# Modulation and other 1024-wide vectors: loaded once as sixteen rows and spread by TensorE, instead of sixteen broadcast loads

## The chip, the cores and the metric

The kernel runs on one core of a Trainium2 chip. The time is the device time of one launch in microseconds (us); the kernel before has a median of 4399.28 us over three runs (4392.77 to 4406.4). The profiled execution took 4396.59 us, of which the profile's span covers 4394.8 us.

## The reference

Two layers of a diffusion backbone run over 128 context tokens and 512 latent tokens (640 rows of width 1024, float32; five tiles of 128 tokens, tile 0 context, tiles 1 to 4 latents). Layer 0 is a mixer (attention and RWKV), layer 1 a Conformer convolution module. Each layer ends with PEER, an expert retrieval: eight heads pick sixteen experts each for every token, so 128 experts of 16384, and each expert has a row `u` and a row `v` of 1024 floats. What this change touches are the vectors of 1024 that are the same for every token:

```python
sp1, cp1, gp1, sp2, cp2, gp2 = modulation(c_ctx[None, :], mod_w[layer], mod_b[layer])   # context
ss1, cs1, gs1, ss2, cs2, gs2 = modulation(c, mod_w[layer], mod_b[layer])                # latents
...
yp = mixer_odd(hp, *prm)                      # ends with "@ w_pw2 + b_pw2"
xp = xp + gp1 * yp
hp = modulate(rmsnorm(xp, norm_g[layer, 1]), sp2, cp2)     # h * (1 + scale) + shift
xp = xp + gp2 * peer(hp, *pprm)
y_prompt = rmsnorm(xp, final_g)
```

and the same for the latents. `peer` gathers `u_tab[eidx]` and `v_tab[eidx]`: sum over the 128 picks of gate * gelu(u . x) * v.

## The kernel before

`phase_mixer_even` (the first 885 us) computes layer 0's mixer and stores all modulation vectors in a DRAM tensor, `K.modrows` (two streams by twelve vectors of 1024). `phase_trunk` does the rest. Its backbone is ten jobs: PEER of layer 0 for tiles 0 to 4 (jobs 0 to 4) and of layer 1 for the same tiles (jobs 5 to 9). A job is 128 picks. For each pick GpSimd issues an indirect DMA that gathers one 8 KB row (u and v) for each of 128 tokens, 1 MB in all, into one of the eight slots of `ring` (L1602). VectorE takes the dot product with h (L1733), ScalarE makes gelu, weight and a diagonal matrix (L1893, L1898, L1904), TensorE multiplies the diagonal with the v half and accumulates over the job in PSUM (L2300 to L2303), and that frees the slot: GpSimd waits for it (`used`) before it issues the next gather.

Everything else of the trunk runs beside the picks, in order written out by hand: a `Side` is a generator that yields ticks, and each engine runs its sides up to tick r before its own work of pick r. VectorE does so at every pick, ScalarE and TensorE at every second. So a step at tick 40 on TensorE stands behind TensorE's pick 39, and a step at tick 42 on VectorE behind its dot product of pick 41. SyncE, which issues the ordinary loads, has no picks: it runs through its sides as far as its semaphore waits let it, and whatever it waits for holds every later load of its list.

The vectors of 1024 are used by VectorE with tokens on partitions, so each must be present on all 128 partitions. Before, each is a DMA with `partition_broadcast(P)`, a read of 128 times 4 KB from DRAM. There are sixteen:

- four into `nrows`, a part of the ring, at the trunk's start (`load_row`, L152): scale and shift of layer 0's PEER for both streams. `modulate_all` on VectorE (L1636, L1638) waits for them, tile 0 for two and tile 1 for two, and makes h of the five tiles.
- four into `grow` (L1554): the gate of PEER, for jobs 0, 1, 5 and 6, used in `add_up` (L1744, L1746) at tick 2 of the next job. For jobs 1, 5 and 6 SyncE waits for `summed` before it.
- one of `cv_b_pw2` and three of gate, scale and shift for tile 0 into `lrow` (L1537, L1539), in job 4, among the loads of `w_pw2`; and three of the latents into the same places (L1544), behind a wait for tile 0's h.
- `final_g` into `lrow` at the end of job 8 (L1584), used in `finish` (L1846).

The step of layer 1 between convolution and PEER is `post(p)`, in jobs 4 (tiles 0 and 1), 6 (tiles 2 and 3) and 8 (tile 4). TensorE multiplies by `w_pw2` in eight blocks at ticks 24 to 38 (L2235); each block's weights are one load of 512 KB into one of two buffers `wq`. Then VectorE adds the bias (`mix`, tick 41, L1818), multiplies by the gate (L1821), adds to x (L1824), after the norm applies scale (L1834) and shift (L1837), and TensorE transposes (tick 52, L2244). The second tile of a pair follows `later` ticks behind: 12 in job 4, 4 in job 6. Then come sixteen query blocks with a load of 512 KB each (L1511).

At the trunk's start ScalarE squares all five tiles and takes five roots (L1882, L1886), the last root waiting for VectorE's work on tile 2; only then does it copy the transposed h out of PSUM (`turned`, L2031), TensorE makes the context tile's queries (L2109) and scores (L2122), VectorE picks the first head's experts (`select`), and GpSimd starts its first gather.

## Time and profile before

| | |
|---|---|
| median of three runs | 4399.28 us |
| profiled execution | 4396.59 us |
| its span | 4394.8 us |
| mixer phase | 0 to 885 us |
| trunk up to the first gather | 887 to 919 us |
| ten jobs | 936 to 4388 us |
| TensorE busy, VectorE busy | 72%, 62% of the span |
| mean DMA rate over the span | 342 GB/s |

How to read the rows further down. PE is TensorE's matmuls, PEld its weight loads, DVE VectorE, ACT ScalarE, POOL GpSimd, SP SyncE; SPq is SyncE issuing a DMA. A line of the page cuts the span into 40 slices, with the busy share in tenths. A line of the table of stages holds: stretch and its length; busy time and instructions of PE, PEld, DVE, ACT, POOL; the granted TensorE clock (1.00 is 2.4 GHz, 0.50 is 1.2 GHz); the DMA engines' mean busy share; and GB/s moved. The stretches for jobs begin with the first dot product of each job. A line of the timeline holds start, length, engine, line, operation, output<-inputs, shape, count, and in brackets how long the engine had been idle and what released it. The profile records a float32 matmul as two instructions, a transpose as one; a count of matmuls in a row is of such records. A line of DMA issues holds destination<-source, the issuing queue, count, size of each and the median time from issue to landing.

### The profile page before, as it was taken

Reading aid. Unit: us, or ns where it says so; the run is one execution under the profiler, and the core shown is the slowest. Engines: PE = TensorE matmul, PEld = TensorE weight load, DVE = VectorE, ACT = ScalarE, POOL = GpSimd, SP = SyncE. Lnnn points to the kernel's source line nnn. Section 1 sums busy time; section 2 is a strip of 40 time slices with the busy share of each in tenths; the row PEclk is TensorE's granted clock in tenths of the full one; section 3 lists DMA queues with packets and bytes.
Section 4 is the critical chain, followed back from the end, with each engine's and each line's share of the span. In section 5 each row is a group of like instructions: output and inputs, shape, how many; then the busy total and the mean of one; then the engine's idle time right before and its main releaser. Section 6 shows DMA issues by size and latency. Waiting matters only on the chain.

```text
span 4394.8 us, 68645 instructions
## 1 busy us (share of the span) xinstructions
PE 3150.5 (72%) x25323; PEld 1501.5 (34%) x25323; DVE 2743.9 (62%) x6925; ACT 1604.0 (36%) x4949; POOL 1471.2 (33%) x1298
## 2 busy tenths in 40 slices
...
DMA  5153000179999999999999999999999999999998
GB/s 227 53 209 123 15 7 4 49 287 367 406 401 421 421 421 414 420 419 418 406 417 390 398 419 420 419 418 418 394 418 420 421 420 414 419 419 419 412 421 336
DMA packets 228988, 1505.07 MB, mean 342 GB/s; under 512 B 32198, under 2 KB 33313, under 8 KB 58289
## 3 DMA queue, kind: packets, MB, share of 16 engines
...
q10 hardware_dynamic: 442, 0.12, 0.0%
...
## 4 chain that ended last, share of the span: by engine, by line
DMA 46%; PE 16%; DVE 8%; ACT 5%; issue 3%; POOL 2%; SPq 0%; ACTq 0%; POOLq 0%; PEldq 0%; DVEq 0%
DMA t_ring<-in_peer_uv,t_eidx 44%; PE t_ps L2300 9%; DVE t_ring L1733 6%; POOL t_ring L1602 2%; PE t_ps L2206 2%; ACT t_dg L1904 1%; DMA t_wq<-in_cv_w_pw 1%; ACT t_wgt L1898 1%; PE t_ps L2109 1%; PE t_ps L2188 1%; PE t_ps L2235 1%; PE t_ps L2265 1%; ACT t_wgt L1893 1%; PE t_ps L2301 0%; DVE t_early L1796 0%
## 5 line engine op out<-in xcount | busy, mean ns | idle before, releaser
L1602 POOL DMA_INDIRECT t_ring<-in_peer_uv,t_eidx x1280 | 1463.7, 1143 | 2890.7 <-PE t_ps L2303 1828.7
L2300 PE MATMUL t_ps<-t_ring,t_dg 64*64 64x512 f32 x2560 | 1573.6, 746 | 1037.6 <-ACT t_dg L1904 1006.5
L1733 DVE SCALAR_TENSOR_TENSOR t_ring<-t_ring,t_hring 128x1024 f32<-128x1024 f32 x1024 | 1255.1, 1226 | 792.2 <-DMA t_ring<-in_peer_uv,t_eidx 789.8
L2303 PE MATMUL t_ps<-t_ring,t_dg 64*64 64x512 f32 x2560 | 1591.3, 754 | 0.0
L2302 PE MATMUL t_ps<-t_ring,t_dg 64*64 64x512 f32 x2560 | 1591.0, 753 | 0.0
L2301 PE MATMUL t_ps<-t_ring,t_dg 64*64 64x512 f32 x2560 | 1590.7, 753 | 0.0
L2300 PEld LDWEIGHTS t_ps<-t_ring,t_dg 64*64 64x64 f32 x2560 | 345.7, 156 | 2036.8 <-issue 2005.0
L1893 ACT ACTIVATE t_wgt<-t_dots 128x2 f32<-128x2 f32 x640 | 130.2, 204 | 1954.8 <-DVE t_ring L1733 1954.1
L1733 DVE SCALAR_TENSOR_TENSOR t_ring<-t_ring,t_early 128x1024 f32<-128x1024 f32 x256 | 314.8, 1230 | 248.3 <-DMA t_ring<-in_peer_uv,t_eidx 248.2
L1904 ACT ACTIVATE t_dg<-t_eye,t_wgt 128x64 f32<-128x64 f32 x1280 | 376.1, 340 | 1.4 <-ACT t_wgt L1898 0.9
L2303 PEld LDWEIGHTS t_ps<-t_ring,t_dg 64*64 64x64 f32 x2560 | 346.8, 156 | 0.0
L2301 PEld LDWEIGHTS t_ps<-t_ring,t_dg 64*64 64x64 f32 x2560 | 346.6, 156 | 0.1
L2302 PEld LDWEIGHTS t_ps<-t_ring,t_dg 64*64 64x64 f32 x2560 | 346.4, 156 | 0.0
L1898 ACT ACTIVATE t_wgt<-t_wgt,t_gate 128x1 f32<-128x1 f32 x1280 | 307.3, 286 | 40.0 <-DVE t_gate L1708 14.5
L2206 PE MATMUL t_ps<-t_early 128*128 128x256 f32 (+1 forms) x930 | 188.3, 355 | 0.0
L2206 PEld LDWEIGHTS t_ps<-t_early 128*128 128x128 f32 x930 | 153.2, 193 | 68.3 <-ACT t_early L1960 38.5
L318 PE MATMUL fr_ps<-ev_hT,ev_wring 128*128 128x512 f32 x336 | 174.3, 601 | 0.0
L2188 PE MATMUL t_ps<-t_early,t_wg 128*128 128x256 f32 (+1 forms) x768 | 154.9, 355 | 5.5 <-DMA t_wg<-in_cv_w_pw 3.2
L1893 ACT ACT_TABLE_LOAD x116 | 148.8, 1283 | 12.6 <-DVE t_ring L1733 10.6
L2265 PE MATMUL t_ps<-t_early,t_wq 128*128 128x256 f32 (+1 forms) x768 | 152.7, 354 | 0.0
L2188 PEld LDWEIGHTS t_ps<-t_early,t_wg 128*128 128x128 f32 x768 | 127.0, 194 | 64.7 <-issue 44.2
L1960 ACT ACTIVATE t_early<-ident,vec 128x128 f32<-128x128 f32 x465 | 145.1, 387 | 1.5 <-PE t_ps L2206 0.6
...
## 6 DMA issues: line engine op xcount, KB each, us to landing
...
t_ring<-in_peer_uv,t_eidx POOLq DMA_INDIRECT x1280, 13.7
...
ev_qk<-in_ab_w_out SPq DMA_DIRECT2D x1, 4096.0 KB, 12.1
...
```

The costliest lines, as they stand in the source:

```text
L1602: pool.indirect_dma_start(ring[:, place[n], :], None, table, bass.IndirectOffsetOnAxis(ap=eidx[:, s % 2, r:r + 1], axis=0)).then_inc(row_i ...
L1733: V.scalar_tensor_tensor(ring[:, place[n], 0:D], ring[:, place[n], 0:D], 1.0, h_of(j), ALU.mult, ALU.mult, accum_out=dots[:, j % 2, r:r + ...
L1893: nc.scalar.activation(wgt[:, r:r + 2], dots[:, j % 2, r:r + 2], ACT.Gelu).then_inc(S["gelu_done"], 1)
L1898: nc.scalar.activation(wgt[:, r + b:r + b + 1], wgt[:, r + b:r + b + 1], ACT.Copy, scale=gate[:, j % 2, r + b:r + b + 1]).then_inc(S["wgt_ ...
L1904: nc.scalar.activation(dg[:, n % DIAGS, :], eye[:], ACT.Copy, scale=wgt[:, r + b:r + b + 1]).then_inc(S["diag_set"], 1)
L2188: last = nc.tensor.matmul(banks[:, 4 + b % 2, 2 * a * P:2 * a * P + N], wg[:, a, k, :], rhs, start=(k == 0), stop=(k == KD - 1))
L2206: nc.tensor.matmul(tiles_of(banks[:, 4 + b % 2, :], p), diag[:, n % BATCH, :], windows(p, b, w), start=(w == 0), stop=(w == CONVW - 1)).th ...
L2265: last = nc.tensor.matmul(tiles_of(banks[:, 6 + b % 2, :], p), wq[:, n % 2, k, :], both[:, k, 0:E, :], start=(k == 0), stop=(k == KD - 1))
L2300: nc.tensor.matmul(straight[low], diagonal[low], row[low, 0:512], **ends)
L2301: nc.tensor.matmul(straight[high], diagonal[high], row[high, 0:512], **ends)
L2302: nc.tensor.matmul(crossed[high], diagonal[low], row[low, 512:D], **ends)
L2303: nc.tensor.matmul(crossed[low], diagonal[high], row[high, 512:D], **ends).then_inc(S["used"], 1)
```

## The change

`load_rows` reads the sixteen vectors once, one per partition, into a tile `rows` of 16 partitions, in six small DMAs at the trunk's start. Where a vector is needed on 128 partitions, TensorE multiplies a column of the identity, repeated 128 times as the stationary operand (16 x 128), with `rows` (16 x 512, twice), which leaves the vector on all partitions in PSUM. VectorE reads it there; only the gate of PEER is copied by ScalarE into `grow`. The bias of `w_pw2` is added by two more matmuls per tile into the same accumulation. As VectorE can read one operand from PSUM, ScalarE copies the product of `w_pw2` to SBUF (`product`) first. Ticks and semaphores are laid out anew, the query blocks of job 4 start at tick 66 instead of 72 and those of job 8 have a step of 3 from tick 66. At the start the transposes use two banks in turn instead of four, since the spread rows hold the others, and the latents' rows are spread after the transposes of tile 0.

```diff
+ROWS = 16
+def row_at(stream, layer, kind):
+    return 7 * stream + (kind + 1 if layer else kind - 3)
+def load_rows(eng, K, rows, sem):
+    for s in range(2):
+        for layer, first, at in ((0, 3, 0), (1, 2, 3)):
+            src = K.modrows[s, (layer * 6 + first) * D:(layer * 6 + 6) * D].rearrange("(r d) -> r d", d=D)
+            eng.dma_start(rows[7 * s + at:7 * s + at + 6 - first], src).then_inc(sem, 16)
+    eng.dma_start(rows[14:15], K.io["cv_b_pw2"]).then_inc(sem, 16)
+    eng.dma_start(rows[15:16], K.io["final_g"].rearrange("(a d) -> a d", a=1)).then_inc(sem, 16)
...
-    later = lambda p, e: (12, 4, 0)[p] * e
-    query_tick = lambda p, b: (72 + 3 * b, 66 + 3 * b, 60 + 7 * b // 2)[p]
-    ahead = lambda p: (12, 14, 14)[p]
+    later = lambda e: 4 * e
+    query_tick = lambda p, b: 66 + 3 * b
+    gate_tick = lambda j: 14 if j else 96
...
-        turned_bank = lambda n: (0, 1, 4, 5)[n % 4]
+        turned_bank = lambda n: n % 2
...
+        def after_product(p):
+            return sorted((at + later(e), n, kind, e) for n, (kind, at) in enumerate((("scale", 44), ("gate", 40), ("shift", 50), ("turn", 54)))
+                          for e in range(len(PAIRS[p])))
...
# SyncE
-                        if k == 2 and p == 0:
-                            sp.dma_start(lrow[:, 3, :], io["cv_b_pw2"][0].partition_broadcast(P)).then_inc(S["lrow_in"], 16)
-                            for a, kind in enumerate((2, 4, 3)):
-                                sp.dma_start(lrow[:, a, :], mod_row(0, kind).partition_broadcast(P)).then_inc(S["lrow_in"], 16)
-                    if p == 0:
-                        yield 51
-                        sp.wait_ge(S["h2_done"], 1)
-                        for a, kind in enumerate((2, 4, 3)):
-                            sp.dma_start(lrow[:, a, :], mod_row(1, kind).partition_broadcast(P)).then_inc(S["lrow_in"], 16)
-                def gate_row(j, tick):
-                    yield tick
-                    if j:
-                        sp.wait_ge(S["summed"], j)
-                    sp.dma_start(grow[:], mod_row(tile(j), 5, j // NT).partition_broadcast(P)).then_inc(S["grow_in"], 16)
-                for s in range(2):
-                    for j, kind in enumerate((4, 3)):
-                        load_row(sp, K, nrows[:, s, j, :], s, 0, kind, rows_in[s])
+                load_rows(sp, K, rows, S["rows_in"])
-                    if s == JOBS - 2:
-                        sp.wait_ge(S["h2_done"], NT)
-                        sp.dma_start(lrow[:, 0, :], io["final_g"].partition_broadcast(P)).then_inc(S["g_in"], 16)
...
# VectorE
                         if t < 2:
-                            dve.wait_ge(rows_in[t], 32)
-                        V.scalar_tensor_tensor(h_of(t), x[:, t, :], rstd[:, t:t + 1], nrows[:, stream(t), 0, :], ALU.mult, ALU.mult).then_inc(S["scaled"], 1)
+                            dve.wait_ge(S["nrows_spread"], 2 * (t + 1))
+                        V.scalar_tensor_tensor(h_of(t), x[:, t, :], rstd[:, t:t + 1], ps[:, 2, :], ALU.mult, ALU.mult).then_inc(S["scaled"], 1)
...
-                    yield 41 + later(p, e)
-                    dve.wait_ge(S["w_done"], p + 1)
-                    dve.wait_ge(S["lrow_in"], 16 * (7 if i else 4))
-                    m = own(V.tensor_tensor(y, ps[:, 2 + e, :], lrow[:, 3, :], ALU.add))
-                    yield 42 + later(p, e)
-                    after_own(m)
-                    m = own(V.tensor_tensor(y, y, lrow[:, 0, :], ALU.mult))
-                    yield 43 + later(p, e)
-                    after_own(m)
+                    yield 42 + later(e)
+                    dve.wait_ge(S["product_out"], i + 1)
+                    dve.wait_ge(S["post_spread"], 3 * PAIRS[p][0] + spread_at(p, "gate", e))
+                    V.tensor_tensor(y, product, ps[:, 1, :], ALU.mult).then_inc(S["gate_read"], 1)
+                    yield 43 + later(e)
+                    dve.wait_ge(S["gate_read"], i + 1)
                     V.tensor_tensor(x[:, i, :], x[:, i, :], y, ALU.add).then_inc(S["mixed"], 1)
...
+                    dve.wait_ge(S["post_spread"], 3 * PAIRS[p][0] + spread_at(p, "scale", e))
+                    V.scalar_tensor_tensor(h_of(j), x[:, i, :], rstd[:, n:n + 1], ps[:, 2 + e, :], ALU.mult, ALU.mult).then_inc(S["scale_read"], 1)
+                    yield 52 + later(e)
+                    dve.wait_ge(S["scale_read"], i + 1)
+                    dve.wait_ge(S["post_spread"], 3 * PAIRS[p][0] + spread_at(p, "shift", e))
+                    V.tensor_tensor(h_of(j), h_of(j), ps[:, 1, :], ALU.add).then_inc(S["h2_done"], 1)
...
# ScalarE
+                def gate_row(j, n):
+                    for a in range(2):
+                        yield gate_tick(j) + 4 * a + 2
+                        act.wait_ge(S["gate_spread"], 2 * n + a + 1)
+                        if j:
+                            act.wait_ge(S["summed"], j)
+                        nc.scalar.copy(grow[:, a * 512:(a + 1) * 512], banks[:, 3, :]).then_inc(S["gate_set"], 1)
...
+                        yield 40 + later(e)
+                        if e:
+                            act.wait_ge(S["gate_read"], i)
+                        else:
+                            act.wait_ge(S["w_done"], p + 1)
+                        nc.scalar.copy(product, ps[:, 2 + e, :]).then_inc(S["product_out"], 1)
...
# TensorE
-                        if n >= 4:
-                            pe.wait_ge(S["hT_done"], n - 3)
+                        if n >= 2:
+                            pe.wait_ge(S["hT_done"], n - 1)
...
+                def spread(row, outs):
+                    for a, out in enumerate(outs):
+                        last = nc.tensor.matmul(out, ident[0:ROWS, row:row + 1].to_broadcast([ROWS, P]), rows[:, a * 512:(a + 1) * 512], start=True, stop=True)
+                    return last
+                def norm_rows(s):
+                    for a, kind in enumerate((4, 3)):
+                        spread(row_at(s, 0, kind), (banks[:, 4 + 2 * a, :], banks[:, 5 + 2 * a, :])).then_inc(S["nrows_spread"], 1)
+                def gate_row(j, n):
+                    row = row_at(stream(tile(j)), j // NT, 5)
+                    for a in range(2):
+                        yield gate_tick(j) + 4 * a
...
+                        nc.tensor.matmul(banks[:, 3, :], ident[0:ROWS, row:row + 1].to_broadcast([ROWS, P]), rows[:, a * 512:(a + 1) * 512],
+                                         start=True, stop=True).then_inc(S["gate_spread"], 1)
+                def final_row():
+                    yield 4
+                    pe.wait_ge(S["hTb_done"], NT)
+                    spread(15, (banks[:, 4, :], banks[:, 5, :])).then_inc(S["g_spread"], 1)
...
+                    for e in range(E):
+                        for a in range(2):
+                            last = nc.tensor.matmul(ps[:, 2 + e, a * 512:(a + 1) * 512], ident[0:ROWS, 14:15].to_broadcast([ROWS, P]),
+                                                    rows[:, a * 512:(a + 1) * 512], start=False, stop=True)
+                    last.then_inc(S["w_done"], 1)
+                    for tick, _, kind, e in after_product(p):
+                        yield tick
+                        i = members[e]
+                        if kind == "gate":
...
+                            spread(row_at(stream(i), 1, 2), (banks[:, 2, :], banks[:, 3, :])).then_inc(S["post_spread"], 1)
+                        elif kind == "scale":
+                            pe.wait_ge(S["gate_read"], i + 1)
+                            spread(row_at(stream(i), 1, 4), (banks[:, 4 + 2 * e, :], banks[:, 5 + 2 * e, :])).then_inc(S["post_spread"], 1)
+                        elif kind == "shift":
+                            pe.wait_ge(S["gate_read"], members[-1] + 1)
+                            if e:
+                                pe.wait_ge(S["h2_done"], i)
+                            spread(row_at(stream(i), 1, 3), (banks[:, 2, :], banks[:, 3, :])).then_inc(S["post_spread"], 1)
...
+                pe.wait_ge(S["rows_in"], 16 * 6)
+                norm_rows(0)
                 turn(0, 2)
+                norm_rows(1)
```

## Rows read from the trace of the kernel before

**Rows 1.** The page: span, DMA busy tenths in 40 slices, the chain by engine.

```profile
span 4394.8 us, 68645 instructions
DMA  5153000179999999999999999999999999999998
...
DMA 46%; PE 16%; DVE 8%; ACT 5%; issue 3%; POOL 2%; SPq 0%; ACTq 0%; POOLq 0%; PEldq 0%; DVEq 0%
```

**Rows 2.** Busy time by stage, for jobs 3, 4, 6 and 7.

```profile
1972.90:2316.70 343.80, 256.37 (x1609) 130.57 (x1604) 256.64 (x676) 177.46 (x541) 146.89 (x128) 0.90 1.01 414
2316.70:2685.60 368.90, 257.06 (x1465) 118.50 (x1461) 235.44 (x589) 128.86 (x419) 150.01 (x129) 0.88 0.99 404
...
3029.40:3389.60 360.20, 259.94 (x1464) 118.36 (x1468) 236.62 (x589) 127.49 (x419) 147.49 (x128) 0.88 1.00 411
3389.60:3712.60 323.00, 209.03 (x1338) 83.03 (x1330) 242.27 (x658) 143.52 (x500) 145.91 (x127) 0.81 1.01 420
```

**Rows 3.** DMA issues of the whole span, with time to landing.

```profile
t_ring<-in_peer_uv,t_eidx POOLq DMA_INDIRECT x1280, 13.7
...
out<-at_kvtok SPq DMA_DIRECT2D x2, 64.0 KB, 1.7
```

**Rows 4.** SyncE's timeline in job 4, the loads around `w_pw2`.

```profile
2372.77 0.43 SPq L1537 DMA_DIRECT2D t_lrow<-in_cv_b_pw  x1
2373.24 1.43 SPq L1539 DMA_DIRECT2D t_lrow<-modrows  x3
2377.90 41.01 SPq L1535 DMA_DIRECT2D t_wq<-in_cv_w_pw  x5
```

**Rows 5.** Tile wq, 2300 to 2440 us: its matmuls, idle time until loads.

```profile
L2235 PE MATMUL t_ps<-t_wq,t_early x64: 592/592/1222, 2368.7 to 2429.7; 128*128 128x512 f32 x64
...
  DMA t_wq<-in_cv_w_pw: 36.2, 7
```

**Rows 6.** The same, 3020 to 3150 us (job 6).

```profile
  DMA t_wq<-in_cv_w_pw: 12.1, 9
```

**Rows 7.** VectorE's timeline in job 4, the first step of `mix`, both tiles.

```profile
2430.38 1.23 DVE L1818 TENSOR_TENSOR t_early<-t_ps,t_lrow 128x1024 f32<-128x1024 f32 x1 [6.19 <-PEq L2239]
...
2470.69 1.23 DVE L1818 TENSOR_TENSOR t_early<-t_ps,t_lrow 128x1024 f32<-128x1024 f32 x1 [9.22 <-DMA t_lrow<-modrows]
```

**Rows 8.** Busy time in stretches of 10 us of job 4.

```profile
2400.00:2410.00 10.00, 8.95 (x26) 3.46 (x27) 5.57 (x12) 1.63 (x8) 1.15 (x1) 0.67 0.76 301
...
2470.00:2480.00 10.00, 3.69 (x16) 0.89 (x16) 9.31 (x26) 2.07 (x10) 2.60 (x2) 0.58 0.89 340
```

**Rows 9.** Tensor work of 512 columns: timeline around 918 us, clock 1.00.

```profile
917.70 10.57 PE L2109 MATMUL t_ps<-t_ring,t_wq 128*128 128x512 f32 x24 [1.04 <-ACT t_ring L2031]
```

**Rows 10.** Timeline of the trunk's start, all engines.

```profile
886.96 1.75 SPq L152 DMA_DIRECT2D t_ring<-modrows  x4
...
892.48 1.28 DVE L1636 SCALAR_TENSOR_TENSOR t_early<-x,t_rstd,t_ring 128x1024 f32<-128x1024 f32 x1 [2.13 <-DMA t_ring<-modrows]
...
895.08 1.97 PE L2103 MATMUL t_ps<-ident,t_early 128*128 128x128 f32 x8 [12.61 <-DVE t_early L1638]
...
895.22 1.28 DVE L1636 SCALAR_TENSOR_TENSOR t_early<-x,t_rstd,t_ring 128x1024 f32<-128x1024 f32 x1
...
900.69 1.05 ACT L2031 COPY t_early<-t_ps 128x512 f32<-128x512 f32 x2
...
910.31 0.49 DVE L1650 MAX8 t_top<-t_early 128x8 f32<-128x128 f32 x2 [4.47 <-ACT t_early L2053]
...
919.20 1.02 POOL L1602 DMA_INDIRECT t_ring<-in_peer_uv,t_eidx  x1 [909.68 <-DVE t_eidx L1693]
```

**Rows 11.** The chain in order of time, job 9: dot products, next gather.

```profile
4152.23 1.25 DVE t_ring L1733 x2
...
4158.37 14.91 DMA t_ring<-in_peer_uv,t_eidx
```

**Rows 12.** Busy time 902 to 904 us, with the granted clock.

```profile
902.00:904.00 2.00, 2.00 (x10) 2.00 (x11) 1.96 (x3) 0.00 (x0) 0.00 (x0) 0.50 0.02 6
```

76 lines of the change are left out of this document (44 added, 32 removed).

## Prediction

> **What bounds the kernel now.** I read the page first. In the 40 slices the DMA digits are 7 or less up to slice 9 and 9 in slices 10 to 39, and DMA is the largest part of the chain, 46% [rows 1]. So there are two parts: a mixer phase that the change leaves alone, and the trunk from 887 us on. Next, the table by job. Job 7 has no ordinary loads: 128 picks in 323.0 us, DMA share 1.01 at 420 GB/s. Job 3 has sixteen loads of 512 KB beside the same picks and takes 343.8 us, also at full share. The difference, 20.8 us, is 1.30 us for a load; 524,288 bytes at 420 GB/s are 1.25 us. Against 323.0 us TensorE has 209 us and VectorE 242 us of work in job 7 [rows 2]. The trunk is bound by bytes: a load that is taken out of a job gives its 1.25 us back, and an operation added on TensorE or ScalarE costs nothing as long as ring slots come free in time. How much time there is for that: a gather lands 13.7 us after its issue [rows 3], while at 420 GB/s its 1 MB takes 2.5 us, so some five gathers are queued. The engines could be late by several microseconds before DMA runs dry.
>
> Job 4 breaks the rule. It has 29 ordinary loads (6 of `w_pw2`, 16 for the queries, 7 into `lrow`), so 323.0 + 29 * 1.25 = 359.3 us were due, and it took 368.9, at a share of 0.99. Job 6, with 25 loads and due at 354.3, took 360.2 [rows 2]. Job 4 loses 9.6 us, job 6 5.9.
>
> **The loads that go.** Four of the sixteen stand at the trunk's start, before the gathers; they are not byte savings. Twelve stand in jobs: seven in job 4, one each for the gates of jobs 0, 1, 5 and 6, and `final_g` in job 8. 12 * 1.25 = 15.0 us; at 1.30 it would be 15.6. A lower bound leaves out the load of job 0, the one job I don't take as byte-bound throughout: 13.8. I take 15.0.
> The Trainium skill (DMA: Bandwidth & Descriptors, Anatomy of one DMA) gives a DMA about 2.0 us plus bytes / 436e3. By that fixed part each load would be worth 3.2 us, 38 us in all. The trace doesn't agree: sixteen loads cost 20.8 us, not 51 [rows 2]; the fixed part is hidden while other transfers are queued.
>
> **Job 4's stalls.** The four loads of 512 KB into `lrow` are issued together, at 2372.8 to 2374.7 us, right ahead of the remaining blocks of `w_pw2`, which take until 2418.9 [rows 4]. TensorE then sits 36.2 us for `wq` in this stretch [rows 5], against 12.1 us for the same work of job 6 [rows 6]. VectorE waits 6.2 us behind it at the first step of `mix`, and for the second tile 9.2 us for the latents' rows [rows 7]. DMA runs partly empty at both places: shares of 0.76 and 0.89 in stretches of 10 us [rows 8], 2.4 + 1.1 = 3.5 us. That is about what job 4 loses more than job 6 (9.6 - 5.9 = 3.7). With the `lrow` loads gone I take -4 us. Ends: 0, if what is late next (the blocks of `w_pw2`, as in job 6) stalls as long; -9.6, if job 4 comes to what is due. SyncE also stops waiting for `summed` and for tile 0's h; the loads behind those waits go out earlier, with the same bytes, and job 6's blocks of `w_pw2` can be there before their tick. I give that nothing.
>
> **The new work beside the picks.** A float32 matmul is two records: 64 records for the 32 matmuls of job 4's `w_pw2` [rows 5]. 24 records of 512 columns take 10.57 us at a clock of 1.00 [rows 9], so a matmul takes 0.88 us there and 1.76 at 0.50. Per tile of `post` there are 2 for the bias and 6 for gate, scale and shift, 40 in five tiles; with 8 for PEER's gates and 2 for `final_g` 50 in all, 44 to 88 us of TensorE over jobs in which it has over 70 us free each [rows 2]. ScalarE gets five copies of 1024 columns and eight of 512, by 1.05 us for two of 512 [rows 10] 9.5 us. VectorE loses five additions of 1.23 us [rows 7], 6.2 us. As busy time all this lies under the DMA: zero.
>
> The waits are another matter. VectorE now waits at tick 42 (gate, spread by TensorE at tick 40, two picks or 5 us before), at 48 (scale, tick 44) and at 52 (shift, tick 50). From the end of a dot product to the next gather lie 4.9 us with two picks' matmuls between (4158.37 - 4153.48) [rows 11]; the two matmuls of a spread add 1.8 to 3.5. So the shift is there 6.7 to 8.4 us after dot 49, while VectorE comes 5.0 after it: a wait of 1.7 to 3.4 us. For the first gate, tick 38 also holds the last block of `w_pw2` and the bias, 7 us for a pair, and ScalarE waits for `w_done` before its copy, with its weights and diagonals behind it; for the second gate TensorE has scale and gate in a row. I put these two waits at 5 us each and the two shifts at 2.5: 15 us for a pair, about half for tile 4, 37 in all, less 6.2 us of additions. Behind VectorE's wait stand its dot products, and with them every slot. Of a pair's 15 us most is hidden: the 6.2 and 9.2 us waits of job 4 cost 3.5 us of DMA together [rows 7, 8]. At that ratio, 3.5 / 15.4, 37 us would cost 8.4; less the relief, I take +6. Ends: 0 (TensorE comes in time) and +25 (30.8 us, most of it felt, because the waits stand within sixteen picks).
>
> **The start.** Here nothing covers. Before, VectorE begins tile 0 at 892.48 us, 5.5 us after the first issue, and tile 1 at 895.22 [rows 10]. Now six issues of 0.44 us (four took 1.75 [rows 10]) end at 889.6, and a small load lands after 1.7 us [rows 3]: the rows are there at 891.3. TensorE makes four matmuls, 3.5 us at a clock of 1.00, 7.0 at 0.50. VectorE's tile 0 takes 2.6 us, TensorE transposes (1.97 us for eight [rows 10], or half), then spreads the latents' rows (3.5 or 7.0). Fast: 891.3 + 3.5 + 2.6 + 1.0 + 3.5 = 901.9, 6.7 us later than 895.2. Slow: 891.3 + 7.0 + 2.6 + 2.0 + 7.0 = 909.9, 14.7 later. The delay arrives at the first gather: ScalarE copies the transposes, at 900.69, only after its last root, which waits for VectorE's tile 2; then come queries, scores, the selection from 910.31 and the gather at 919.20, each waiting for the one ahead [rows 10]. VectorE's own end of the five tiles (about 906 us) has 4.5 us of slack before 910.31 and moves with the rest. The granted clock was 0.50 at 902 to 904 us, when the queries began [rows 12]. I take 0.50 for the first four matmuls in part, 5.5 us, and 1.00 from then on: 891.3 + 5.5 + 2.6 + 1.0 + 3.5 = 903.9, +8.7. The queries then run at 1.00 too, and the first of them, sixteen records, takes 1.8 instead of 3.5 us: -1.5. So +7; ends 5 and 15. Two banks instead of four for the latents' transposes lie behind the chain to the first gather: zero, or 1 us.
> The Trainium skill (TensorE: Matmul & The Clock Gate, Part 1: The HAM clock gate) says that the array runs at 1.2 GHz after idling until it has been kept busy. By that alone the first spread would be the slow one, 7.0 us, and the start +8.5.
>
> **The sum.** -15.0 - 4 + 6 + 7 = -6 us on the profiled execution's 4396.59, so 4390.6. This execution lies 2.7 us under the median of the runs; for the median, 4399.3 - 6 = 4393.3, given as 4393.
>
> **Rivals.** (1) More comes back: job 4 loses nothing any more (-9.6 instead of -4), job 6 gains 3 us from earlier loads, no new wait is felt (0) and the start costs 5: -15.0 - 9.6 - 3 + 5 = -22.6, 4377. For it: SyncE is released from four waits. Against it: job 6 loses 5.9 us without any `lrow` load.
> (2) Slower than before: the handoffs at ticks 38 to 58 of jobs 4, 6 and 8. If the waits of a pair add up to more than the queued gathers hold (five, of 2.5 us), DMA runs dry at each of the five tiles by 7 us: 35 in place of the 6, so +23, 4422. It makes the kernel slower from (6 + 6) / 5 = 2.4 us of lost DMA time a tile on. For it: such waits emptied the DMA before [rows 7, 8], and now four stand close together. Against it: the longest of them, 9.2 us, lost 1.1.
> (3) The loads weren't what the jobs paid for; they filled gaps that gathers can't use. Then the twelve give 0: -4 + 6 + 7 = +9, 4408. Against it: job 3 against job 7 [rows 2].
> (4) A load holds the DMA engines for a fixed time besides its bytes: 1.7 us, what a small load takes [rows 3]. Then each of the twelve gives 1.7 us more, 20.4 in all: -26.4, 4373. Against it: job 3 against job 7, 1.30 us for a load with everything in it [rows 2]. This is the rule of the Trainium skill's DMA page named above.
>
> **How the numbers follow.** Forecast 0.65, rival 1 0.12, rival 2 0.13, rival 3 0.07, rival 4 0.03. About 0.3% of the time, 13.2 us, is what a measurement of this kernel can tell from no change. The forecast's bounds, -15.6 - 9.6 + 0 + 5 = -20 and -13.8 + 0 + 25 + 15 = +26 at the outside, put 0.09 of its 0.65 past -13.2 and 0.05 past +13.2. So faster 0.12 + 0.03 + 0.09 = 0.24, slower 0.13 + 0.05 = 0.18, same 0.58. The range that leaves out 2 in 10 reaches at the low end almost to rival 1, 4378, at the high end past rival 3, 4412.
>
> **What would show it.** The table by job: job 4 at 350 to 358 us, jobs 0, 1 and 5 about 1.2 us shorter, job 7 at 323. The first gather at 924 to 929 us. TensorE's wait for `wq` in job 4 near 12 us. VectorE idle until TensorE or ScalarE at the gate's product, some 5 us each. I would be wrong if jobs with one load less stayed as long as before, if DMA shares fell under 0.9 at ticks 38 to 58 of jobs 4, 6 and 8, or if the first gather came before 922 or after 935 us.

## The result, and the profile after

The changed kernel has a median of 4406.39 us, the kernel before, in runs beside it, 4398.19. The ratio is 1.0021, 95% interval 1.0014 to 1.0028: slower by 9.2 us (8.2 by the medians), where 6 us faster was forecast. The time lies in the stated range, and the difference within the 0.3% (13.2 us) that the prediction took for the least that can be told from no change. With 22 runs of each kernel the interval is 0.07% to either side, so the difference is clear of zero; in the experiments, with 4 to 12 runs, it is 0.08 to 0.15%. The sign was wrong, and the two terms that make it so can be named. The profiled execution took 4404.7 us, 8.1 more than that of before.

The page (span, DMA busy tenths in 40 slices, the chain by engine):

```profile
span 4402.9 us, 68889 instructions
DMA  5152000159999999999999999999999999999998
...
DMA 41%; PE 21%; DVE 8%; ACT 4%; issue 4%; POOL 2%; SPq 0%; ACTq 0%; POOLq 0%; PEldq 0%; DVEq 0%
```

Against [rows 1] the chain has five hundredths less of DMA and five more of TensorE. Slice 9 is emptier: the gathers begin later. All slices after it are as full as before, which says that the page is too coarse for what follows.

A correction first, which holds for [rows 2] as well: the stretches there start 11.7 us after each job's first dot product, not with it, and so does the "936" of the table of times (the first dot product is at 924.7 us). Both ends of a stretch are off by the same amount, so the lengths, on which everything rests, are those from first dot product to first dot product. The table of after is cut in the same way, 11.9 us behind. Also, the DMA issues of job 6's stretch are 27 ordinary loads, not 25 (16 for the queries, 10 of `w_pw2`, one for the gate); at 1.25 us each 356.8 us were due there and 3.4 were lost, not 5.9.

Busy time by stage after (columns as in [rows 2]), jobs 3, 4, 6 and 7:

```profile
1986.10:2330.00 343.90, 258.37 (x1606) 131.88 (x1602) 256.92 (x676) 175.45 (x541) 152.82 (x128) 0.89 1.01 414
2330.00:2694.20 364.20, 283.04 (x1496) 125.71 (x1492) 233.17 (x587) 129.25 (x420) 150.50 (x128) 0.85 0.99 402
...
3037.00:3400.10 363.10, 283.27 (x1500) 126.65 (x1493) 233.02 (x587) 130.18 (x421) 143.85 (x128) 0.87 0.99 404
3400.10:3723.10 323.00, 214.95 (x1342) 84.64 (x1346) 244.78 (x665) 145.24 (x506) 144.55 (x128) 0.79 1.01 420
```

Jobs 3 and 7, which the change hardly touches, are as long as before within 0.2 us. Job 4 has 24 loads for 29 and is 4.7 us shorter; 6.25 were due for the bytes alone. Job 6 has 24 for 27 and is 2.9 us longer. The rest, from first dot product to first dot product: job 0 +4.6 us (its gate load is gone, but it has three loads more, 1 MB of keys and two of weights that waited for `summed` in job 1 before), job 1 -6.1, job 5 -1.0, job 8 -1.3, jobs 2 and 9 unchanged. In sum the ten jobs give -5.4 us, all that lies ahead of the first dot product (924.7 us before, 939.3 after) +14.5, the end -1.0: +8.1.

The start, all engines in order (timeline; columns as in [rows 10]):

```profile
886.27 1.20 SPq L163 DMA_DIRECT2D t_rows<-modrows  x4
889.26 7.19 PE L2130 MATMUL t_ps<-t_rows,ident 16*128 16x512 f32 x8 [7.47 <-DMA t_rows<-in_final_g]
896.56 1.28 DVE L1642 SCALAR_TENSOR_TENSOR t_early<-x,t_rstd,t_ps 128x1024 f32<-128x1024 f32 x1 [6.90 <-PE t_ps L2130]
899.14 1.97 PE L2125 MATMUL t_ps<-ident,t_early 128*128 128x128 f32 x8 [2.70 <-DVE t_early L1644]
901.04 7.19 PE L2130 MATMUL t_ps<-t_rows,ident 16*128 16x512 f32 x8
908.35 1.28 DVE L1642 SCALAR_TENSOR_TENSOR t_early<-x,t_rstd,t_ps 128x1024 f32<-128x1024 f32 x1 [9.12 <-PE t_ps L2130]
913.79 1.05 ACT L2052 COPY t_early<-t_ps 128x512 f32<-128x512 f32 x2
...
933.55 1.02 POOL L1608 DMA_INDIRECT t_ring<-in_peer_uv,t_eidx  x1 [924.03 <-DVE t_eidx L1699]
```

The mixer phase differs by some microseconds from one execution to the next, so I read the start from SyncE's first issue of the trunk. Before, the first gather is 32.2 us behind it [rows 10], now 933.55 - 886.27 = 47.3: +15.0. VectorE reaches tile 1 22.1 us behind the issue instead of 8.3, +13.8, and ScalarE's copy, which waits for VectorE's tile 2 through the last root, is later by the same 13.8. From the copy to the first gather it takes 19.8 us instead of 18.5: the queries begin at a granted clock of 0.50 here too, and it is back at 1.00 from 922 us on, 8 us behind the copy; before it was so from 906, 5 us behind. Both spreads of the start took 7.19 us, at half the clock (busy time by stage of the two stretches, granted clock third from the end):

```profile
889.00:897.00 8.00, 7.19 (x8) 2.46 (x8) 0.70 (x3) 2.63 (x8) 0.00 (x0) 0.50 0.97 376
901.00:908.30 7.30, 7.24 (x9) 2.49 (x8) 0.00 (x0) 0.00 (x0) 0.00 (x0) 0.50 0.00 0
```

Job 4 on VectorE: the steps that replaced those of [rows 7] (timeline), and what the new waits come to over the whole span (for the lines L1824 and L1842, the engine's idle time before them in us, and how often):

```profile
2434.64 1.22 DVE L1824 TENSOR_TENSOR t_early<-t_early,t_ps 128x1024 f32<-128x1024 f32 x1 [2.13 <-PE t_ps L2130]
...
2452.27 1.22 DVE L1824 TENSOR_TENSOR t_early<-t_early,t_ps 128x1024 f32<-128x1024 f32 x1 [7.85 <-PE t_ps L2130]
...
2471.90 1.22 DVE L1842 TENSOR_TENSOR t_hring<-t_hring,t_ps 128x1024 f32<-128x1024 f32 x1 [3.32 <-PE t_ps L2130]
...
2485.83 1.22 DVE L1842 TENSOR_TENSOR t_hring<-t_hring,t_ps 128x1024 f32<-128x1024 f32 x1 [4.00 <-PE t_ps L2130]
```

```profile
  PE t_ps L2130: 19.4, 4
```

```profile
  PE t_ps L2130: 17.2, 5
```

The two lines are the product with the gate and the addition of the shift. Together 36.6 us (17.3 in job 4, 16.7 in job 6, 2.6 in job 8), all of them until TensorE's spread; 37 were forecast. The longest in job 4 is that of the second gate, 7.85 us: TensorE spreads the first tile's scale and the second tile's gate in a row, and does so at half the clock (TensorE's timeline, then busy time in stretches of 10 us of job 4):

```profile
2444.98 7.19 PE L2130 MATMUL t_ps<-t_rows,ident 16*128 16x512 f32 x8
```

```profile
2440.00:2450.00 10.00, 8.64 (x22) 3.04 (x23) 4.35 (x14) 4.29 (x13) 3.21 (x3) 0.50 1.01 421
2450.00:2460.00 10.00, 7.26 (x27) 1.74 (x29) 5.26 (x11) 2.53 (x7) 2.01 (x2) 0.50 0.87 338
2460.00:2470.00 10.00, 10.00 (x33) 2.73 (x26) 8.38 (x20) 5.26 (x15) 3.13 (x4) 0.50 0.85 294
...
2480.00:2490.00 10.00, 10.00 (x36) 3.80 (x32) 5.97 (x17) 1.28 (x6) 2.19 (x3) 0.50 0.69 259
2490.00:2500.00 10.00, 7.88 (x64) 2.66 (x56) 9.96 (x26) 5.22 (x17) 7.92 (x7) 0.97 0.85 316
```

TensorE is busy for whole stretches at 0.50, and the DMA share falls to 0.69. It is still 1.01 in the stretch in which VectorE begins its wait for the second gate, and 0.69 to 0.96 in all that follow up to 2500 us; in job 6 it goes the same way, 1.01 or more up to 3160 us and 0.73 to 0.90 from there to 3200. In job 8, with one tile and one wait of 2.6 us, no stretch of 10 us around the step is under 0.99. The stretches of before around the same steps had 0.76 and 0.89 [rows 8]. The stall on `wq` is gone from job 4, though (tile wq from 2330 to 2440 us, TensorE's idle time until its loads):

```profile
  DMA t_wq<-in_cv_w_pw: 11.5, 10
```

11.5 us where there were 36.2 [rows 5].

### The profile page after: what moved, and what is told of

The parts are those of the page before. It is cut to its first block, busy times and chain, and to the rows that moved or that the text cites. A ratio compares the mean times of both kernels' runs of the same rounds, so it can differ in the third digit from the quotient of the medians.

```text
span 4402.9 us, 68889 instructions
## 1 busy us (share of the span) xinstructions
PE 3241.4 (74%) x25439; PEld 1533.7 (35%) x25439; DVE 2738.4 (62%) x6920; ACT 1610.2 (37%) x4961; POOL 1475.2 (34%) x1298
## 4 chain that ended last, share of the span: by engine, by line
DMA 41%; PE 21%; DVE 8%; ACT 4%; issue 4%; POOL 2%; SPq 0%; ACTq 0%; POOLq 0%; PEldq 0%; DVEq 0%
DMA t_ring<-in_peer_uv,t_eidx 40%; PE t_ps L2376 10%; DVE t_ring L1739 5%; POOL t_ring L1608 2%; PE t_ps L2158 2%; PE t_ps L2255 2%; PE t_ps L2237 1%; ACT t_dg L1909 1%; PE t_ps L2130 1%; ACT t_wgt L1903 1%; PE t_ps L2284 1%; DMA t_wq<-in_cv_w_pw 1%; PE t_ps L2335 1%; ACT t_wgt L1898 1%; PE t_ps L2377 0%
## 5 line engine op out<-in xcount | busy, mean ns | idle before, releaser
L2376 PE MATMUL t_ps<-t_ring,t_dg 64*64 64x512 f32 x2560 | 1591.4, 754 | 966.7 <-ACT t_dg L1909 925.4
L2379 PE MATMUL t_ps<-t_ring,t_dg 64*64 64x512 f32 x2560 | 1608.4, 761 | 0.0
L2378 PE MATMUL t_ps<-t_ring,t_dg 64*64 64x512 f32 x2560 | 1608.0, 761 | 0.0
L2377 PE MATMUL t_ps<-t_ring,t_dg 64*64 64x512 f32 x2560 | 1607.7, 760 | 0.0
L1903 ACT ACTIVATE t_wgt<-t_wgt,t_gate 128x1 f32<-128x1 f32 x1280 | 307.2, 286 | 38.9 <-DVE t_gate L1714 13.1
```

The costliest lines, as they stand in the source:

```text
L1903: nc.scalar.activation(wgt[:, r + b:r + b + 1], wgt[:, r + b:r + b + 1], ACT.Copy, scale=gate[:, j % 2, r + b:r + b + 1]).then_inc(S["wgt_ ...
L2376: nc.tensor.matmul(straight[low], diagonal[low], row[low, 0:512], **ends)
L2377: nc.tensor.matmul(straight[high], diagonal[high], row[high, 0:512], **ends)
L2378: nc.tensor.matmul(crossed[high], diagonal[low], row[low, 512:D], **ends)
L2379: nc.tensor.matmul(crossed[low], diagonal[high], row[high, 512:D], **ends).then_inc(S["used"], 1)
```

## The experiments

The theory after the result: the start costs 15 us, as much as the bytes give, and the new waits of VectorE in `post` cost more than the share I gave them. The rivals: the bytes gave less than 15 us, or some other part of the new order costs the time. All results are ratios to the kernel before in runs beside it. The kernels leave nothing of the computation out; two add unused work, as told there. The number beside "first gather" is its distance from SyncE's first issue of the trunk.

**1. The start alone, from both sides.** `a_start_loads` is the changed kernel with the old start: four broadcast loads for `nrows`, four banks for the transposes.

```diff
...
+                for s in range(2):
+                    for j, kind in enumerate((4, 3)):
+                        load_row(sp, K, nrows[:, s, j, :], s, 0, kind, nrows_in[s])
                 load_rows(sp, K, rows, S["rows_in"])
...
-                pe.wait_ge(S["rows_in"], 16 * 6)
-                norm_rows(0)
                 turn(0, 2)
-                norm_rows(1)
+                pe.wait_ge(S["rows_in"], 16 * 6)
```

> The changed kernel with the start as before: the four broadcast loads into the ring, four banks for the transposes; everything else of the change stays. My theory (the start alone costs 15 us, the jobs give 5.5 us net): first gather 14.5 us earlier than in the changed kernel, span about 4388 us, ratio to before 0.998 to 0.999. Rival (the start's delay is absorbed in job 0, which isn't bound by bytes, and the loss lies in the jobs): span stays near 4400 us, ratio 1.000 to 1.002.

Measured: 0.9990 (0.998 to 1.0), first gather 32.5 us. `b_start` is the kernel before with the new start alone:

```diff
...
-                for s in range(2):
-                    for j, kind in enumerate((4, 3)):
-                        load_row(sp, K, nrows[:, s, j, :], s, 0, kind, rows_in[s])
+                load_rows(sp, K, rows, S["rows6_in"])
...
+                pe.wait_ge(S["rows6_in"], 16 * 6)
+                norm_rows(0)
                 turn(0, 2)
+                norm_rows(1)
```

> The kernel before with the start of the change alone (rows loaded in six small loads, spread by TensorE, two banks for the transposes, the latents' rows after tile 0's transposes). My theory: the first gather 14 to 15 us later than in the kernel before and all of it at the end: ratio 1.0033. Rival (absorbed in job 0): ratio 1.000 to 1.001 with job 0 shorter by 10 us.

Measured: 1.0029 (1.0018 to 1.0041), first gather 46.1 us. So the start costs 0.0029 * 4398 = 12.8 us by the one (7.9 to 18.0 by the interval) and (1.0021 - 0.9990) * 4398 = 13.6 by the other. Both fit the theory, and the rival, that job 0 takes the delay in, falls: job 0 of `b_start` isn't shorter than before but 4.5 us longer, without an added load. So the loads that moved into job 0 need not be what makes it longer in the changed kernel; what does was not looked into. The rest of the change gives 0.0010 * 4398 = 4.4 us (0 to 8.8), of 15 us of bytes.

**2. The bytes.** `a_dead12` adds twelve loads of the removed kind to job 7, into a tile that nobody reads.

```diff
...
+                    if s == 7:
+                        sp.wait_ge(S["summed"], 7)
+                        for n in range(12):
+                            if n:
+                                sp.wait_ge(S["dead_in"], 16 * n)
+                            sp.dma_start(dead[:], mod_row(1, 2).partition_broadcast(P)).then_inc(S["dead_in"], 16)
...
```

> The changed kernel with twelve broadcast loads of 512 KB added in job 7, one after the other, into a tile that nobody reads: the price of a load by itself. My theory (bytes): job 7 grows from 323 us by 12 x 1.25 = 15 us to 338 us, all of it at the end. Rival (the loads fill gaps that gathers can't use): under 4 us. Rival (a load costs its fixed time too): 30 us or more.

Measured: 1.0064 (1.0049 to 1.0078). Job 7 (busy time by stage, and its loads from the DMA issues of the same stretch):

```profile
3392.30:3732.50 340.20, 216.59 (x1342) 85.60 (x1344) 243.79 (x664) 144.74 (x506) 144.27 (x128) 0.80 1.01 420
```

```profile
t_dead<-modrows SPq DMA_DIRECT2D x12, 512.0 KB
...
t_wq<-in_cv_w_pw SPq DMA_DIRECT2D x2, 512.0 KB
```

It is 340.2 us long with fourteen loads (two blocks of `w_pw2` came along into it) where it had been 323.0 with none: 17.2 / 14 = 1.23 us for a load, at the same 420 GB/s. The rival that the bytes gave less falls, and so does a fixed price per load besides its bytes. The Trainium skill (DMA: Bandwidth & Descriptors, Anatomy of one DMA) has about 2.0 us of fixed time in each DMA, measured for DMAs that GpSimd issues. For these loads, which SyncE issues beside the gathers, no part of it is seen in the throughput: 1.23 us a load, where the bytes alone make 1.25.

**3. The start's clock and order.** `a_warm` puts 64 records of unused matmuls behind the mixer's last one and two groups of twelve matmuls around the first spread, to see the same spreads at the full clock.

```diff
...
+                for n in range(12):
+                    nc.tensor.matmul(banks[:, 0, 0:P], ident[:], ident[:], start=True, stop=True)
                 pe.wait_ge(S["rows_in"], 16 * 6)
                 norm_rows(0)
+                for n in range(12):
+                    nc.tensor.matmul(banks[:, 0, 0:P], ident[:], ident[:], start=True, stop=True)
...
+                pe.wait_ge(gated, 3)
+                for n in range(32):
+                    nc.tensor.matmul(ps[:, 2, 0:P], K.ident[:], K.ident[:], start=True, stop=True)
```

> The changed kernel with matmuls whose result nobody reads on TensorE: 32 after the mixer's last real ones, 12 before the rows have landed, 12 between the two spreads. My theory (the start costs its 15 us half for the clock of 1.2 GHz, half for the matmuls and the order themselves): the granted clock is 1.00 for the spreads, each of the two takes 3.5 to 4 us in place of 7.2, the first gather comes 6 to 8 us earlier relative to the trunk's first load. Rival (order and handoffs set the start, the clock doesn't): under 2 us.

Measured: 1.0024 (1.0015 to 1.0033), first gather 40.9 us. Timeline, then busy time by stage:

```profile
885.32 7.31 PE L1323 MATMUL wo_ps<-ident 128*128 128x128 f32 x64
...
897.44 3.70 PE L2133 MATMUL t_ps<-t_rows,ident 16*128 16x512 f32 x8 [0.17 <-DMA t_rows<-in_final_g]
...
906.45 3.69 PE L2133 MATMUL t_ps<-t_rows,ident 16*128 16x512 f32 x8
```

```profile
897.40:901.20 3.80, 3.76 (x9) 1.53 (x10) 0.26 (x2) 2.26 (x6) 0.00 (x0) 1.00 0.91 372
```

The same eight records take 3.70 us at 1.00 and 7.19 at 0.50. The first gather came 6.4 us nearer; 7.0 us are what the two spreads save. The ratio shows nothing of it: the unused matmuls behind the mixer took 7.31 us themselves, and the trunk's first issue comes at 894.3 us, 8.0 later than in the changed kernel's profile. As that issue lies anywhere from 877.8 to 890.5 us in the other kernels' profiles, that they held the trunk's beginning is likely, not shown. So the clock makes 6.4 of the start's 15.0 us, and warming it up in this place pays nothing.

`a_both` spreads the rows of both streams in one go, into eight banks, so that VectorE's tile 1 no longer waits for a second round.

```diff
...
                 norm_rows(0)
-                turn(0, 2)
                 norm_rows(1)
+                turn(0, 2)
```

> The changed kernel with one order altered: both streams' rows are spread at once into all eight banks, ahead of the transposes of tile 0, so that the second spread lies beside VectorE's work on tile 0. My theory: the second spread (7.2 us) goes off the path but the transposes of tile 0 wait for what is left of it; tile 1 begins 7 to 9 us earlier, the first gather 7 to 9 us earlier than in the changed kernel, ratio to before 1.0000 to 1.0005. Rival (TensorE's halved clock, not the order, sets the start): under 3 us.

Measured: 1.0019 (1.001 to 1.0028), first gather 41.4 us, 5.9 nearer. That is short of the 7 to 9 us of the theory and twice the rival's 3, and the ratio, expected at 1.0000 to 1.0005, did not move beyond its interval. TensorE's timeline and busy time by stage:

```profile
885.74 14.02 PE L2130 MATMUL t_ps<-t_rows,ident 16*128 16x512 f32 x16 [7.56 <-DMA t_rows<-in_final_g]
```

```profile
885.70:899.70 14.00, 13.96 (x17) 5.16 (x17) 2.89 (x6) 3.57 (x10) 0.00 (x0) 0.50 0.55 222
```

Fourteen microseconds of matmuls without a gap stayed at 0.50, and the transposes of tile 0 had to wait for them. `b_both` is the same edit on `b_start`:

> b_start (the kernel before with the new start alone, ratio 1.0029) with both streams' rows spread at once ahead of tile 0's transposes. First gather 5 to 6 us earlier than in b_start. My theory: ratio 1.0015 to 1.0018. Rival (job 0 absorbs it): 1.0029 as b_start, job 0 longer by 5 us.

Measured: 1.0028 (1.0017 to 1.0038), first gather 41.5 us, 4.6 nearer than in `b_start`. From the trunk's first issue to the end of the span there are 3519.7 us against 3524.8 in `b_start`: in the profiled execution the gain arrives at the end, in the ratio, expected at 1.0015 to 1.0018, it can't be told from nothing. Job 0, which by the rival would be 5 us longer, is 3.4 shorter.

`a_turn_first` leaves TensorE alone and lets ScalarE copy the transposes before the last square and the last two roots, so that the copy no longer waits for VectorE's tile 2.

```diff
...
                 for t in range(NT + 1):
                     if t < NT:
+                        if t == NT - 1:
+                            turned(0, 2)
                         square(h_of(t), t, t)
                     if t:
                         root(t - 1)
...
-                turned(0, 2)
```

> The changed kernel with one thing moved on ScalarE: the copy of tile 0's transposes stands ahead of the square of tile 4 and the last two roots instead of behind them. My theory (the delay of the latents' tiles reaches the first gather only through ScalarE's last root): the queries now wait for TensorE alone, which is done with the second spread 15.5 us before it was the roots' turn ends; the first gather comes 4 to 6 us earlier relative to the trunk's first load than the changed kernel's 47.4. Rival (the path runs through VectorE's own work on the five tiles): under 1 us.

Measured: 1.002 (1.0009 to 1.0031), first gather 41.5 us, 5.8 nearer, as the theory had it; the ratio is that of the changed kernel. `b_turn_first` is this edit on the kernel before:

> The kernel before with ScalarE's copy of tile 0's transposes ahead of the last square and roots, nothing of the change. The first gather comes 4 to 5 us earlier, as in best2 against best1. My theory (a shift of the first gather arrives at the end in full): ratio 0.9990. Rival (job 0, held up by TensorE's latent scores, absorbs it, and only a delay of the latents' tiles arrives): ratio 0.9998 to 1.0002 with job 0 longer by 4 us.

Measured: 0.9985 (0.9976 to 0.9994), first gather 28.7 us instead of 32.2. 3.6 us nearer, 6.6 us faster (2.6 to 10.6 by the interval). So the last root was on the path of the start in both kernels. That a shift of the first gather reaches the end of the kernel is clear where it is large (the 15 us of `b_start`) and agrees with this run; the four other small shifts (`a_warm`, `a_both`, `b_both`, `a_turn_first`, 4.6 to 6.4 us) can't be told from nothing in their ratios.

**4. The waits in `post`.** `a_early` adds the bias first and the blocks of `w_pw2` onto it, and spreads the first gate at tick 22, long before its use.

```diff
...
+                    yield 22
+                    pe.wait_ge(S["scaled1"], p + 1)
...
+                            nc.tensor.matmul(ps[:, 2 + e, a * 512:(a + 1) * 512], ident[0:ROWS, 14:15].to_broadcast([ROWS, P]),
+                                             rows[:, a * 512:(a + 1) * 512], start=True, stop=False)
+                    spread(row_at(stream(members[0]), 1, 2), (banks[:, 2, :], banks[:, 3, :])).then_inc(S["post_spread"], 1)
                     for k in range(KD):
                         yield 24 + 2 * k
```

> The changed kernel with two steps of post moved ahead: the bias matmuls open the accumulation of w_pw2 instead of closing it, and the first gate is spread at tick 22 instead of 40. My theory (DMA time is lost where VectorE waits, and the largest wait, 7.9 us at the second gate behind scale and gate in a row, stays): VectorE's wait at the first gate goes, 2.1 us in job 4 and 1.6 in job 6; jobs 4 and 6 get 1 to 3 us shorter together. Rival (what counts is TensorE's lateness from tick 38 on, through the bias): each of jobs 4 and 6 gets back its whole loss of 4 to 5 us.

Measured: 1.0015 (1.0007 to 1.0024). VectorE's two gate products of job 4 (timeline):

```profile
2434.10 1.22 DVE L1824 TENSOR_TENSOR t_early<-t_early,t_ps 128x1024 f32<-128x1024 f32 x1 [3.43 <-ACT t_early L2007]
...
2446.66 1.22 DVE L1824 TENSOR_TENSOR t_early<-t_early,t_ps 128x1024 f32<-128x1024 f32 x1 [2.78 <-PE t_ps L2130]
```

The theory had it the other way round: the first wait was to go and the second to stay. The second gate's wait fell from 7.85 to 2.8 us: the first scale and the second gate are still spread in a row, but the eight records took 3.85 us at a mean clock of 0.94, not 7.19 at 0.50. The first waits 3.4 us for ScalarE's copy of the product instead of TensorE; that copy, which the change added, is the next bound there. Jobs 4 and 6 are 2.9 us shorter together, as the theory said (1 to 3), and the rival's 4 to 5 us for each did not come. The interval overlaps that of the changed kernel.

`a_reuse` doesn't spread a vector again for the second tile of job 6, whose two tiles are both latents: three spreads instead of six.

```diff
...
                         i = members[e]
+                        if e and kind != "turn" and stream(i) == stream(members[0]):
+                            issued = 3 * members[0] + spread_at(p, kind, e) - 1
+                            pe.wait_ge(S["post_spread"], issued)
+                            pe.sem_inc(S["post_spread"], 1)
+                            continue
```

> The changed kernel, where both tiles of a pair are latents (job 6) gate, scale and shift are spread once and read twice: 3 spreads in place of 6. Job 4 (a context tile and a latent tile) keeps its 6 and is the control. My theory (DMA time is lost because VectorE waits for TensorE's spreads): job 6 loses 3 to 5 us less than in the changed kernel, about 4 us, as before the change, while job 4 keeps its 8 to 13 us of lost DMA time. Rival (the two added matmul pairs for the bias and ScalarE's copy are what makes everything late): job 6 changes by under 1.5 us.

Measured: 1.0014 (1.0005 to 1.0023). Job 6 took 363.6 us against 363.1, where the theory wanted 3 to 5 less. But its waits did not fall either, 17.0 us against 16.7, so the run decides neither for the theory nor for the rival, and the interval overlaps that of the changed kernel.

`s_swap` is `a_start_loads` with the second gate spread ahead of the first scale:

```diff
...
-(("scale", 44), ("gate", 40), ("shift", 50), ("turn", 54))
+(("gate", 40), ("scale", 44), ("shift", 50), ("turn", 54))
...
```

> The kernel with the old start (a_start_loads, ratio 0.999) with one order altered in post: at tick 44 the second tile's gate is spread ahead of the first tile's scale. My theory: VectorE's longest wait, 7.9 us at the second gate, falls to about 4; each of jobs 4 and 6 gets 1.5 to 3 us back; ratio 0.998. Rival (the first tile's scale, now late, makes up for it): no change, 0.999.

Measured: 0.9993 (0.9984 to 1.0002), where `a_start_loads` had 0.9990. The second gate's wait fell to 4.5 us, as expected, and in the profiled executions jobs 4 and 6 together are 12.3 us shorter than in `a_start_loads`; the ratio does not show it. Its expected value, 0.998, missed, and it warns against reading one execution alone.

**5. All repairs together.** `best1` is `a_start_loads` with the edits of `a_early`, `a_reuse` and `s_swap`; `best2` adds `a_turn_first`; `best3` keeps the whole change (no broadcast load at all) with `a_both` and all of the others.

> The changed kernel with the start by four loads as before, the bias first and the first gate at tick 22, the second gate ahead of the first scale, and spreads read twice where both tiles are latents. My theory (15 us of bytes, less what the waits lose): start as before, jobs 4 and 6 lose 5 to 7 us each, so the whole is 10 to 14 us under the kernel before, ratio 0.997. Rival (the loss in jobs 4 and 6 comes from elsewhere): ratio 0.999 as with the old start alone.

> best1 (ratio 0.9966) with ScalarE's copy of tile 0's transposes moved ahead of the last square and roots. My theory: the first gather comes 3 to 4 us earlier, ratio 0.996. Rival (job 0, which TensorE holds up, absorbs it): 0.9966 as before.

> The change kept whole, without a broadcast load, but with all repairs: both streams' rows spread at once, ScalarE's copy of tile 0's transposes ahead of the last roots, bias first, first gate at tick 22, second gate ahead of the first scale, spreads read twice where both tiles are latents. My theory: the start costs 4 to 5 us over the kernel before instead of 15, jobs as in best1, ratio 0.9975 to 0.998. Rival (whatever else of the change costs time, the six small loads or two banks for the transposes): ratio over 0.999.

Measured: `best1` 0.9966 (0.9952 to 0.998), first gather 33.6 us; `best2` 0.9964 (0.9951 to 0.9978), 28.8 us; `best3` 0.9986 (0.9975 to 0.9996), 37.6 us. `best1` gives 15.0 us (8.8 to 21.1 by the interval), as much as the bytes of twelve loads, and 10.6 more than `a_start_loads`, from which it differs only in the handoffs of `post`. So those handoffs cost time, and the rival that the loss in jobs 4 and 6 comes from elsewhere falls. Jobs 4 and 6 of `best1` (busy time by stage), and its gate products in job 4 (timeline):

```profile
2300.90:2662.00 361.10, 278.65 (x1496) 124.78 (x1497) 233.95 (x586) 129.14 (x419) 147.96 (x128) 0.87 0.99 405
3005.50:3366.10 360.60, 281.09 (x1488) 126.24 (x1492) 233.43 (x586) 129.94 (x422) 155.23 (x128) 0.86 1.00 407
```

```profile
2418.32 1.22 DVE L1829 TENSOR_TENSOR t_early<-t_early,t_ps 128x1024 f32<-128x1024 f32 x1 [2.34 <-ACT t_early L2012]
2430.66 1.22 DVE L1829 TENSOR_TENSOR t_early<-t_early,t_ps 128x1024 f32<-128x1024 f32 x1 [2.19 <-PE t_ps L2135]
```

`best2` has the lowest ratio of all, median 4379.86 us, some 16 us under the kernel before; `best1`, median 4378.79, can't be told from it. `best3` shows that even with every repair the start by TensorE costs about 0.0022 * 4398 = 9.7 us against `best2` and its start by loads; its first gather is 8.8 us later.

**6. How much of VectorE's waits is felt.** `after_again` is the changed kernel once more, for its scatter:

> The changed kernel once more, for a second profile of the same code beside the others. My theory (jobs 4 and 6 lose more or less by which clock level the spreads meet): the lengths of jobs 4 and 6 differ from the first profile's 364.2 and 363.1 us by several microseconds, up to 370, with VectorE's waits for the spreads; all other jobs within 1 us but job 0. Rival (the same code gives the same lengths, and the longer jobs of the variants come from what they changed): both within 1.5 us.

Measured: 1.0024 (1.0013 to 1.0036), jobs 4 and 6 at 366.7 and 364.4 us. The same code is 2.5 and 1.3 us longer there than in its first profile: less than the theory's several microseconds, more than the rival's 1.5 in one of the two. So differences of this size between two kernels of the table below can be chance. Now the table over all kernels. "Lost" is the length of jobs 4 and 6 less 2 * 323.0 and less 1.25 us for each of their loads (56 before, 48 in most others; the DMA issues of the stretches give the count). The waits are VectorE's idle time in these two jobs ahead of its gate and shift steps (before: ahead of the first step of `mix`, [rows 7]; the same for the other kernels with the old `post`).

| kernel | `post` | jobs 4, 6 (us) | waits | lost |
|---|---|---|---|---|
| before | old | 368.9, 360.2 | 15.7 | 13.1 |
| `b_turn_first` | old | 366.3, 360.6 | 16.3 | 10.9 |
| `b_start`, `b_both` | old | 368.9, 361.5; 370.4, 360.0 | 14.7, 16.7 | 14.4, 14.4 |
| after | new | 364.2, 363.1 | 34.0 | 21.3 |
| `after_again` | new | 366.7, 364.4 | 36.4 | 25.1 |
| `a_reuse` | job 6 less | 367.8, 363.6 | 36.2 | 25.4 |
| `a_dead12` | new | 369.9, 359.1 | 35.6 | 25.5 |
| `a_turn_first` | new | 364.6, 369.2 | 37.4 | 27.8 |
| `a_start_loads` | new | 367.2, 367.0 | 38.8 | 28.2 |
| `a_both`, `a_warm` | new | 367.2, 370.7; 367.3, 370.7 | 42.0 | 31.9, 32.0 |
| `s_swap` | order | 361.7, 360.2 | 26.0 | 15.9 |
| `a_early` | early | 361.3, 363.1 | 24.3 | 18.4 |
| `best1` | all | 361.1, 360.6 | 20.7 | 15.7 |
| `best2` | all | 362.5, 357.2 | 20.1 | 13.7 |
| `best3` | all | 364.4, 357.7 | 20.8 | 16.1 |

From about 20 us of waits to 42 the loss goes from about 15 to 32: 17 / 22, about 0.8 us lost for each microsecond of wait. This is a slope through one profile of each kernel, in which waits and loss go together; that the waits are the whole of the loss is not shown. In job 6 of the four kernels with the old `post` VectorE waits 0.3 us at most, and 3.3 to 4.8 us are lost all the same. Job 8, on the other hand, whose single tile has 2.6 to 5.0 us of waits in the kernels with the new `post`, is as long as its loads make it, within 1.6 us. The seven kernels with the new `post` unchanged lose 27.4 us on average, the four with the old one 13.2: 14 us. Within the intervals this agrees with the ratios, which know nothing of this table: the change without its start gave 4.4 us, 10.6 less than the bytes.

## Why the prediction was right or wrong

- **The loads that go, -15.0.** Right. 1.23 us for a load in `a_dead12`, and `best1` gives back 15.0 us.
- **Job 4's stalls, -4.** That job 4 of before loses 9.6 us was read rightly; the 5.9 us of job 6 were 3.4, so the difference that was held against the 3.5 us of idle DMA was 6.2, and the agreement came of the miscount. The stall went as forecast: TensorE's wait for `wq` is 11.5 us, "near 12" in the prediction. What this gave in time can't be separated from the new waits that stand in the same picks; `best2`, with the new `post` and 20.1 us of waits, loses 13.7 us, no less than before with 15.7 us of waits (13.1), so the relief looks small.
- **The new work beside the picks.** As busy time it costs nothing, as said: job 7 and job 3 are unchanged. The size of VectorE's waits was right too, 36.6 us for 37.
- **The share of the waits that is felt: this step failed.** "At that ratio, 3.5 / 15.4, 37 us would cost 8.4; less the relief, I take +6." The ratio came from two waits of before, in one execution, read from two stretches of 10 us with a DMA share under one; the stretch from 2360 to 2370 us, with 0.80, was not among them. By the prediction's own count job 4 lost 9.6 us beside these 15.4 us of waits. The runs show about 0.8, not 0.23. I had seen that five gathers of 2.5 us are queued, and took it for a cover for each wait anew. The rows above read better as one cover for all: in jobs 4 and 6 DMA is full up to the second wait and not afterwards, and in job 8, with one wait, always. Why it stays short, by my reading because jobs bound by DMA fill the queue again only slowly, no run tests by itself. The prediction said "most of it felt, because the waits stand within sixteen picks" at the upper end of its range, and that end was nearer. Relief and waits together were put at +2; they are +8.2 in the profiled execution of after (21.3 - 13.1) and 14 on average.
- **The start, +7: this step failed as well.** "I take 0.50 for the first four matmuls in part, 5.5 us, and 1.00 from then on." It was 0.50 for both spreads, 7.19 us each; the first gather came 15.0 us later, the slow end ("14.7 later" for tile 1, measured 13.8). The 1.5 us that the queries were to give back at a clock of 1.00 did not come either: they began at 0.50, and the way from the copy to the gather is 1.2 us longer than before. The row that spoke for it stood in the prediction: 0.50 at 902 to 904 us [rows 12]. That the delay arrives in full at the first gather, through the last root and the copy, was right, and `b_turn_first` shows that path by itself. The Trainium skill (TensorE: Matmul & The Clock Gate, Part 1: The HAM clock gate) says that the array is at half rate after idling until it has been kept busy. The trace agrees in that the first spread, which followed 7.47 us of idle time, ran at 0.50. It doesn't agree in the rest: that spread was busy for 7.19 us without a gap, the one of `a_both` for 14.02, and neither brought 1.00. The measurement decides.
- **The sum.** On the profiled execution: -15.0, then +8.2 in jobs 4 and 6, +14.5 up to the first dot product, +1.4 in the other jobs, -1.0 at the end, +8.1 in all. Two terms, forecast at 7 and 2, were 7.5 and 6.2 too small, which is nearly all of the 14 us between -6 and +8.1. One of the prediction's signs of being wrong came true, DMA shares of 0.69 to 0.87 at the steps of `post`; the first gather, at 933.6 us, just missed another, 935. Job 4, 364.2 us, lies above the 350 to 358 that the forecast wanted. That the time still lies in the range owes to its width and is no merit of the mechanism: both errors go the same way, and each stays within its upper end (15 for the start, 25 for the waits).
- **The rivals.** Rival 2, slower through the handoffs in `post`, named the right mechanism. It wanted 35 us lost there, 7 for each of five tiles; the 8.2 to 14 us of jobs 4 and 6, what the stall gave already taken off, are a quarter to two fifths of that. Rivals 3 and 4 fall by `a_dead12`. In rival 1, job 4 did not come to what was due.

Two things stay open. Why job 6 took 363 to 364 us with the new `post` where the first gather was late (after, `after_again`, `a_reuse`, `a_early`), and 367 to 371 where it was early (`a_start_loads`, `a_both`, `a_warm`, `a_turn_first`), isn't settled; its wait for the first gate was 1.5 or 1.7 us in after and `after_again`, 4.8 to 8.7 in the four with an early first gather, but 7.7 in `a_reuse`. When the last block of `w_pw2` landed and whether the spread met a clock of 1.00 (1.98 us) or 0.50 (3.78 us) go into it; why they should go with the start was not found. It may be why the 6 us that `a_both` and `a_turn_first` gain at the start don't appear in their ratios; 0.1% of interval is 4.4 us, so that may also be all there is to it. The other: how much of the 0.8 us is due to the waits themselves and how much to what made TensorE and ScalarE late; the spread of after and `after_again`, 21.3 and 25.1 us lost by the same code, is too wide to part them.
